# Other starting bytes in SBUF for the operands of 14,600 matmuls

## The chip, the core and the metric

The kernel runs on one core of a Trainium2 chip. The metric is the device time of one execution in microseconds. Of the kernel before there are three such times, 2232.58, 2233.57 and 2234.03 us; their median is 2233.57 us. A profiled execution gives the trace from which all rows below are read; its first to last instruction take 2229.6 us.

## The reference, cut to what matters

Two transformer blocks of two layers each run over the same 256 tokens of 1,024 values. Almost all the arithmetic is products of the activations with weight matrices that are used once:

```
def swiglu(x, w_gu, w_down):
    gate, up = jnp.split(x @ w_gu, 2, axis=-1)
    return (jax.nn.silu(gate) * up) @ w_down

def memory_cross_attention(x, mem, wq, wkv, wo):
    q = (x @ wq).reshape(B_, S, X_HEADS, X_HEAD_DIM) * (X_HEAD_DIM ** -0.5)
    k, v = jnp.split(mem @ wkv, 2, axis=-1)
    ...
    return o.reshape(B_, S, D_MODEL) @ wo
```

The first block has an mLSTM and neighbourhood mixer (layer 0), a differential attention (layer 1), and in each layer a cross attention and a SwiGLU of 2,816 hidden units. Each layer of the second block has a SwiGLU, a mixer of three branches with gates (the name merge in the code), a cross attention and a second SwiGLU. Layer norm with a residual stands after each of the 14 sublayers. All is in float32.

## The kernel before, in words

**Split operands.** TensorE multiplies at its fast rate in a float32 variant (F32R) with fewer bits. To keep accuracy, each operand is held as a high part and a low part: xh and xl are the transposed activations of a sublayer's input, hh and hl those of the hidden units, oh and ol those of an attention's or mixer's output, mh and ml those of the memory, yh and yl those of the three branches. A weight tile of 2,048 values a partition (8,192 bytes, 1 MB in all) comes by DMA into one of three buffers `raw`, ScalarE rounds it into `wh` (line 1260), VectorE writes what is left over into `wl` (line 1813), and TensorE makes three matmuls of each product (helper `three`, lines of `mm`, line 359): high by low, low by high, high by high. wh and wl have three buffers each, which are given back by the semaphore weights_used.

**What moves and what stands.** In proj_T the weights are the stationary operand (128 columns are loaded) and the activations move, 256 columns an instruction. In y_products (the second matrix of a SwiGLU, the output projections) and in proj_N it is the other way round: 128 columns of the activations stand, and 512 (or 256) columns of weights move. In enter, the first tiles of a next sublayer, the activations x stand and 256 or 512 columns of early weight tiles move; those tiles lie in front_h/front_l, in oh/ol (slot "side"), in hh/hl ("back"), or in em_h/em_l and en_h/en_l ("mem", "note", "under"). In a row of the profile `bank<-xl,wh 128x256` is a matmul of xl with wh by 256 moving columns.

**The order.** It is written out by hand: each engine's program calls the same sublayers in the same order, and semaphores join them. Nothing in it depends on addresses.

**Where tensors lie.** SBUF is given out in the order of the calls of sb: each tensor begins where the one before ends, and tensors named gap_... take only room. Tensors in an ExitStack that is closed share their room with what follows. The list begins at byte 16,512 of a partition, which is 128 past a multiple of 2,048 and of 512. From this and from the sizes the homes follow. Below, "remainder" is the starting byte of a tensor modulo 512. Every split tensor's inner steps are multiples of 512 bytes, so that each matmul operand in it starts at the tensor's own remainder.

## Time and profile before

| what | us |
|---|---|
| median of three runs | 2233.57 |
| span of the profiled execution | 2229.6 |
| what lies around the span (the difference) | 4.0 |
| TensorE busy with matmuls | 2202.7 |
| VectorE busy | 1434.7 |
| ScalarE busy | 1074.2 |
| GpSimd busy | 118.6 |

The profiled execution gives only a span; its own whole time is not recorded apart from it, so the 4.0 us are taken as lying around every span. Busy time of TensorE is a union: a matmul of 256 columns is shown as 276 ns long, but the next starts some 113 ns after it. For this kernel the distance from start to start is thus what costs, and it is read by dividing a stretch by its number of matmuls.

### The profile page before, as it was taken

What the parts mean: (1) busy time and instruction counts of PE and PEld (TensorE: products, weight loads), DVE (VectorE), ACT (ScalarE), POOL (GpSimd) and SP (SyncE); (2) the same over time, 40 slices, a digit from 0 to 9 for tenths busy, and PEclk for the clock granted to TensorE, in tenths of its full rate; (3) what the DMA queues carried; (4) which work ended last, traced back from release to release, by engine and by line L of the source; (5) the groups of instructions that cost most, each with busy time, mean ns of one, the idle gap of its engine ahead of it and who ended that gap; (6) DMA issues with size and microseconds to landing.
All of it is one profiled execution on the core that took longest, in us unless ns stands there. A gap on an engine that the chain in (4) does not pass through costs nothing.

```text
span 2229.6 us, 38285 instructions
## 1 busy us (share of the span) xinstructions
PE 2202.7 (99%) x16049; PEld 2048.8 (92%) x16049; DVE 1434.7 (64%) x1675; ACT 1074.2 (48%) x1317; POOL 118.6 (5%) x206
## 2 busy tenths in 40 slices
PE   9999999999999999999999999999999999999998
PEld 9989899888989989998999998998998999998997
DVE  6885655577655555556876676566556776677555
ACT  4554444357454443443556454444443555555442
POOL 2310000020000000000011000000000002000000
PEclk9999999999999999999999999999999999999999
DMA  7656556674645665566454655565565555465553
GB/s 244 213 186 208 169 175 191 203 200 153 208 151 181 198 226 171 189 218 197 151 159 145 198 196 179 193 217 180 189 200 193 180 164 160 153 234 163 189 180 123
DMA packets 349547, 413.93 MB, mean 186 GB/s; under 512 B 11964, under 2 KB 281464, under 8 KB 349248
## 3 DMA queue, kind: packets, MB, share of 16 engines
q1 hardware_dynamic: 339184, 377.19, 52.6%
q0 software_dynamic: 10192, 34.29, 4.8%
q8 instruction: 129, 2.11, 0.4%
q14 instruction: 42, 0.34, 0.0%
HBM read 406.44 MB, written 5.00 MB: 185 GB/s over the span
## 4 chain that ended last, share of the span: by engine, by line
PE 94%; DVE 3%; ACT 1%; issue 1%; DMA 0%; POOL 0%; DVEq 0%; ACTq 0%
PE bank L359 94%; DVE x L1927 0%; DVE z L1922 0%; DVE stat L1888 0%; DVE front_l L1813 0%; DVE z L1886 0%; PE bank L1226 0%; ACT wh L1260 0%; DMA lamt<-in_odd_lambda 0%; DVE em_l L1813 0%; ACT em_h L1260 0%; PE bank L1230 0%; DMA rx<-rs 0%; DVE xl L1847 0%; DVE nmax L2277 0%
## 5 line engine op out<-in xcount | busy, mean ns | idle before, releaser
L1813 DVE TENSOR_TENSOR wl<-raw,wh 128x2048 fp32r<-128x2048 f32 (+1 forms) x344 | 761.2, 2218 | 507.2 <-ACT wh L1260 426.6
L359 PE MATMUL bank<-xl,wh 128*128 128x256 f32 x3144 | 877.3, 279 | 5.4 <-issue 4.7
L359 PE MATMUL bank<-xh,wl 128*128 128x256 f32 x3144 | 871.2, 277 | 0.0
L359 PE MATMUL bank<-xh,wh 128*128 128x256 f32 x3144 | 871.2, 277 | 0.0
L1260 ACT ACTIVATE wh<-raw 128x2048 fp32r<-128x2048 f32 (+1 forms) x344 | 636.7, 1855 | 316.5 <-PE bank L359 306.6
L359 PEld LDWEIGHTS bank<-xl,wh 128*128 128x128 f32 x3144 | 591.7, 188 | 12.5 <-issue 10.5
L359 PEld LDWEIGHTS bank<-xh,wl 128*128 128x128 f32 x3144 | 591.2, 188 | 0.6
L359 PEld LDWEIGHTS bank<-xh,wh 128*128 128x128 f32 x3144 | 591.5, 188 | 0.2
L359 PE MATMUL bank<-wl,hh 128*128 128x512 f32 x528 | 205.9, 390 | 0.0
L359 PE MATMUL bank<-wh,hh 128*128 128x512 f32 x528 | 205.5, 389 | 0.0
L359 PE MATMUL bank<-wh,hl 128*128 128x512 f32 x528 | 205.5, 389 | 0.0
L1448 ACT ACTIVATE gate_s<-bank 128x512 f32<-128x512 f32 x54 | 32.4, 600 | 180.7 <-PE bank L359 180.7
L359 PEld LDWEIGHTS bank<-wh,hh 128*128 128x128 f32 x528 | 99.1, 188 | 20.7
L359 PEld LDWEIGHTS bank<-wh,hl 128*128 128x128 f32 x528 | 99.1, 188 | 20.3
L359 PEld LDWEIGHTS bank<-wl,hh 128*128 128x128 f32 x528 | 99.1, 188 | 20.0
L359 PE MATMUL bank<-wl,oh 128*128 128x512 f32 x224 | 89.7, 400 | 1.8 <-DVE ol L2268 1.6
L359 PE MATMUL bank<-wh,oh 128*128 128x512 f32 x224 | 87.4, 390 | 0.0
L359 PE MATMUL bank<-wh,ol 128*128 128x512 f32 x224 | 87.3, 390 | 0.0
L2546 POOL DMA_DIRECT2D gb<-in_ln_g x14 | 7.6, 543 | 1369.0 <-DVE x L1927 1362.1
L1291 ACT ACTIVATE xh<-bank 128x512 fp32r<-128x512 f32 x56 | 30.8, 600 | 73.3 <-PE bank L359 73.0
L1318 ACT ACTIVATE mv<-mv 128x1 f32<-128x1 f32 x28 | 5.7, 203 | 121.4 <-DVE mv L1914 121.4
L1886 DVE SCALAR_TENSOR_TENSOR z<-x,bank 128x512 f32<-128x512 f32 x56 | 38.3, 684 | 31.4 <-PE bank L359 30.9
(393 smaller groups left out, 3154.5 us busy)
## 6 DMA issues: line engine op xcount, KB each, us to landing
raw<-in_ffn_w_in SPq DMA_DIRECT2D x80, 1024.0 KB, 5.2
raw<-in_w_mix_in SPq DMA_DIRECT2D x56, 1024.0 KB, 5.3
raw<-in_ffn_w_gu SPq DMA_DIRECT2D x40, 1024.0 KB, 5.2
raw<-in_ffn_w_out SPq DMA_DIRECT2D x40, 1024.0 KB, 5.1
raw<-in_ffn_w_down SPq DMA_DIRECT2D x20, 1024.0 KB, 5.1
raw<-in_mem_wkv SPq DMA_DIRECT2D x16, 1024.0 KB, 5.4
raw<-in_even_w_in SPq DMA_DIRECT2D x13, 1024.0 KB, 6.8
raw<-in_w_branch SPq DMA_DIRECT2D x24, 512.0 KB, 3.5
```

The source lines that it names most:

```text
L359: ins = pe.transpose(o, a, b) if transpose else pe.matmul(o, a, b, start=start, stop=stop)
L1260: act.activation(part_of(t, 0), raw_tile(t), ACT.Copy).then_inc(sig("w_high"), 1)
L1291: act.activation(dst, src, ACT.Copy).then_inc(sig("part_high"), 1)
L1318: act.activation(mv[:, t, 2:3], mv[:, t, 1:2], ACT.Sqrt).then_inc(sig("std_ready"), 1)
L1448: free(("gate", j, q), act.activation(gate_s[:, q % 2, :], o[:, :], ACT.Silu))
L1813: dve.tensor_tensor(part_of(t, 1), raw_tile(t), part_of(t, 0).bitcast(F32), ALU.subtract)\
L1886: free(name, dve.scalar_tensor_tensor(z[:, t, f], x[:, t, f], ALPHA / c, o[:, :], ALU.mult, ALU.add))
L2546: pool.dma_start(gb[:, i, :], v.partition_broadcast(P)).then_inc(sig("gains_loaded"), 16)
```

## The change

Only calls of sb are changed: gap tensors are resized, put in or taken out, and seven small tensors move in front of the weights. No instruction is added, removed or moved: of the 21,600 instructions of the built program, on all engines, none differs in its operation, its shape, its operands' names, its offset inside them, or its semaphores. Line numbers below the change shift by two. The highest byte in use rises by 64.

| tensors | remainder by 512 before | after |
|---|---|---|
| wh, wl (all three buffers) | 128 (640 by 2,048) | 0 (0 by 2,048) |
| xh, xl | 64 | 448 |
| hh, hl | 128 | 0 |
| mh, ml; em_h, em_l, en_h | 64 | 0 |
| oh, ol | 128 | 64 |
| en_l | 128 | 64 |
| front_h, front_l | 128 | 0 |
| yh, yl | 64 | 128 |
| raw | 128 | 64 |
| x, z | 128 | 128 |

```
-    sb("gap_xh", [P, 112])
+    sb("gap_xh", [P, 80])
...
-    sb("gap_oh", [P, 16])
+    sb("gap_oh", [P, 32])
...
     raw = sb("raw", [P, RAW, TILE])
+    ident = sb("ident", [P, P])
+    pc = sb("pc", [P, P])
+    stat = sb("stat", [P, TB, 4, 6])
+    mv = sb("mv", [P, TB, 4])
+    nmax = sb("nmax", [P, 2, 4])
+    psum_e = sb("psum_e", [P, 2, 4])
+    rden = sb("rden", [P, 2, 4])
+    sb("gap_wh", [P, 32])
     wh = sb("wh", [P, PARTS, TILE], F32R)
     wl = sb("wl", [P, PARTS, TILE], F32R)
     gb = sb("gb", [P, 2, D])
-    ident = sb("ident", [P, P])
...
-    pc = sb("pc", [P, P])
-    stat = sb("stat", [P, TB, 4, 6])
-    mv = sb("mv", [P, TB, 4])
-    nmax = sb("nmax", [P, 2, 4])
-    psum_e = sb("psum_e", [P, 2, 4])
-    rden = sb("rden", [P, 2, 4])
...
-    sb("gap_hh", [P, 48], F32, st)
...
-    sb("gap_mh", [P, 32], F32, st)
...
-    sb("gap_em", [P, 32], F32, st)
```

The parts of the kernel that the diff touches, and what calls them:

Of the kernel before, what the change touches and what calls it, by code (L numbers as in the profile page):

```python
# [7 lines left out]
F32 = mybir.dt.float32  # L8
# [5 lines left out]
P = 128  # L14
# [3 lines left out]
TB = S // P  # L18
# [63 lines left out]
def program(nc, ctx, A, out, LAST=14):  # L82

    def sb(name, shape, dt=F32, on=None):
        return (on or ctx).enter_context(nc.sbuf_tensor(name, shape, dt))
# [4 lines left out]

    x = sb("x", [P, TB, D])
    z = sb("z", [P, TB, D])
    sb("gap_xh", [P, 112])
    st = ExitStack()
    mem_x = sb("mem_x", [P, TB, D], F32, st)
    st.close()
    xh = sb("xh", [P, KC, S], F32R)
    xl = sb("xl", [P, KC, S], F32R)
    sb("gap_oh", [P, 16])
    st = ExitStack()  # L100
    btab = sb("btab", [8, 512], F32, st)
    st.close()
    st = ExitStack()
# [2 lines left out]
    oh = sb("oh", [P, KC, S], F32R)  # L106
    ol = sb("ol", [P, KC, S], F32R)
    raw = sb("raw", [P, RAW, TILE])
    wh = sb("wh", [P, PARTS, TILE], F32R)
    wl = sb("wl", [P, PARTS, TILE], F32R)  # L110
    gb = sb("gb", [P, 2, D])
    ident = sb("ident", [P, P])
    ones = sb("ones", [P, P])
    st = ExitStack()
    front_h = sb("front_h", [P, TILE], F32R, st)
# [2 lines left out]
    st = ExitStack()  # L118
# [3 lines left out]
    probT = sb("probT", [P, 2, 512])  # L122
    logit = sb("logit", [P, 2, 512])
    bm = sb("bm", [P, 2, 512])
    pc = sb("pc", [P, P])
    stat = sb("stat", [P, TB, 4, 6])
    mv = sb("mv", [P, TB, 4])
    nmax = sb("nmax", [P, 2, 4])
    psum_e = sb("psum_e", [P, 2, 4])
    rden = sb("rden", [P, 2, 4])  # L130


    st = ExitStack()
    sb("gap_hh", [P, 48], F32, st)
    hh = sb("hh", [P, HC, S], F32R, st)
    hl = sb("hl", [P, HC, S], F32R, st)
    gate_s = sb("gate_s", [P, 2, 512], F32, st)
    hid = sb("hid", [P, 2, 512], F32, st)
    st.close()
    st = ExitStack()  # L140
    sb("gap_mh", [P, 32], F32, st)
    mh = sb("mh", [P, KC, S], F32R, st)
    ml = sb("ml", [P, KC, S], F32R, st)
    mem_n = sb("mem_n", [P, TB, D], F32, st)
# [2 lines left out]
    xv = sb("xv", [P, TB, D], F32, st)  # L147
    st.close()
    st = ExitStack()
    sb("gap_em", [P, 32], F32, st)  # L150
    em_h = sb("em_h", [P, TILE], F32R, st)
    em_l = sb("em_l", [P, TILE], F32R, st)
    en_h = sb("en_h", [P, TILE], F32R, st)
# [3 lines left out]
    st = ExitStack()  # L157
# [23 lines left out]
    st = ExitStack()  # L181
# [3 lines left out]
    st = ExitStack()  # L185
# [12 lines left out]
    st = ExitStack()  # L198
# [23 lines left out]
    st = ExitStack()  # L222
# [2515 lines left out]
```

## Rows read from the trace of the kernel before

**Rows 1.** Busy time of each engine, and the chain that ended last, by engine.
```profile
PE 2202.7 (99%) x16049; PEld 2048.8 (92%) x16049; DVE 1434.7 (64%) x1675; ACT 1074.2 (48%) x1317; POOL 118.6 (5%) x206
...
PE 94%; DVE 3%; ACT 1%; issue 1%; DMA 0%; POOL 0%; DVEq 0%; ACTq 0%
```

**Rows 2.** Busy time (instructions), clock, DMA share, GB/s in three stretches.
```profile
core 0: us, PE busy (x) PEld busy (x) DVE busy (x) ACT busy (x) POOL busy (x), PEclk, DMA share, GB/s
277.80:375.90 98.10, 98.10 (x868) 98.10 (x867) 51.26 (x34) 43.30 (x36) 0.00 (x0) 1.00 0.59 187
162.30:184.80 22.50, 22.50 (x192) 22.49 (x191) 17.61 (x17) 9.29 (x8) 1.10 (x2) 1.00 0.83 278
382.00:440.00 58.00, 58.00 (x259) 47.99 (x258) 33.65 (x28) 23.36 (x16) 0.00 (x0) 1.00 0.68 218
```

**Rows 3.** Tile xh, from 277.7 to 375.9: duration ns min/median/max, first and last start.
```profile
L359 PE MATMUL bank<-xh,wl x288: 276/276/279, 277.9 to 375.5; 128*128 128x256 f32 x144
```

**Rows 4.** Tile xh in a slow stretch, from 217.4 to 223.2.
```profile
L359 PE MATMUL bank<-xh,wl x16: 281/281/281, 217.8 to 223.1; 128*128 128x256 f32 x16
L359 PE MATMUL bank<-xh,wh x15: 281/281/281, 217.9 to 222.9; 128*128 128x256 f32 x15
```

**Rows 5.** Tile mh from 162.2 to 184.8, and from 1980 to 1991.
```profile
L359 PE MATMUL bank<-mh,wl x64: 281/281/281, 162.4 to 184.7; 128*128 128x256 f32 x64
...
L359 PE MATMUL bank<-mh,wl x30: 281/281/281, 1980.7 to 1990.9; 128*128 128x256 f32 x30
```

**Rows 6.** Tile yh, from 1221 to 1235.
```profile
L359 PE MATMUL bank<-yh,wl x42: 276/276/276, 1220.8 to 1234.7; 128*128 128x256 f32 x42
```

**Rows 7.** 512 moving columns: tile hh 384.5:440, oh 245:252, mh 151.2:162.2, xh 39:45.
```profile
L359 PE MATMUL bank<-wl,hh x81: 389/389/389, 384.6 to 439.0; 128*128 128x512 f32 x81
...
L359 PE MATMUL bank<-wl,oh x11: 389/389/389, 245.1 to 251.9; 128*128 128x512 f32 x11
...
L359 PE MATMUL bank<-wl,mh x16: 392/392/392, 151.3 to 161.6; 128*128 128x512 f32 x16
L359 PE MATMUL bank<-wh,mh x16: 388/388/389, 151.8 to 162.1; 128*128 128x512 f32 x16
...
L359 PE MATMUL bank<-wh,ml x16: 394/394/394, 151.6 to 161.8; 128*128 128x512 f32 x16
...
L359 PE MATMUL bank<-wl,xh x8: 397/398/400, 39.7 to 44.6; 128*128 128x512 f32 x8
```

**Rows 8.** x standing, 256 columns moving: tiles em_h, front_h 258:277.8; ol 845:857.
```profile
L359 PE MATMUL bank<-em_h,xh x16: 281/283/283, 258.8 to 272.0; 128*128 128x256 f32 x16
...
L359 PE MATMUL bank<-front_h,xh x16: 278/279/279, 266.7 to 277.7; 128*128 128x256 f32 x16
...
L359 PE MATMUL bank<-ol,xh x8: 279/279/279, 853.5 to 856.0; 128*128 128x256 f32 x8
```

**Rows 9.** Groups with shapes apart: busy us, mean ns, idle before.
```profile
L359 PE MATMUL bank<-xh,wl 128*128 128x256 f32 x3136 | 869.0, 277 | 0.0
L1813 DVE TENSOR_TENSOR wl<-raw,wh 128x2048 fp32r<-128x2048 f32 x321 | 734.4, 2292 | 486.0 <-ACT wh L1260 405.6 <-issue 79.7
L359 PE MATMUL bank<-wl,hh 128*128 128x512 f32 x528 | 205.9, 390 | 0.0
L359 PE MATMUL bank<-wl,oh 128*128 128x512 f32 x224 | 89.7, 400 | 1.8 <-DVE ol L2268 1.6
L359 PE MATMUL bank<-mh,wl 128*128 128x256 f32 x192 | 54.0, 281 | 0.0
L359 PE MATMUL bank<-yh,wl 128*128 128x256 f32 x192 | 53.0, 276 | 0.0
```

**Rows 10.** Who waited for whom: TensorE's longest, ScalarE's longest (us, times, longest).
```profile
PE bank L359 <- DVE x L1927: 7.2, 10, 1.4
...
ACT wh L1260 <- PE bank L359: 306.6, 119, 4.4
```

**Rows 11.** DMA issues of weights: count, KB each, median us to landing.
```profile
raw<-in_ffn_w_in SPq DMA_DIRECT2D x80, 1024.0 KB, 5.2
```

## The prediction

> **What bounds the kernel now.** I read the page's busy times and chain first. TensorE is busy 2202.7 of 2229.6 us and is 94% of the chain that ended last [rows 1]: only 26.9 us of the span are not matmuls. The granted clock is 1.00 in every stretch that I cite [rows 2], the level of 2.4 GHz, so it explains no difference below. Next I asked what a matmul costs from start to start. In the SwiGLU from 277.8 to 375.9 us, 98.10 us hold 868 matmuls, nearly all of 256 columns: 113 ns each. In the memory projection, 22.50 us hold 192 matmuls of the same shape: 117 ns each [rows 2]. The tile views say the same more sharply: 288 matmuls xh,wl, every third one, start between 277.9 and 375.5 us, which is 97.6/287/3 = 113.4 ns, each shown as 276 ns long [rows 3]; 64 of mh,wl start between 162.4 and 184.7, 22.3/63/3 = 118.0 ns, each shown as 281 ns long [rows 5]. So 5 ns more of shown duration go with 4.6 ns more from start to start, and the shown durations tell which of the two rates a stretch has.
>
> This is all that a change of addresses could move on the bounding engine, and there is little of it. Above the best rate stand:
> - x moving, weights standing (3 x 3,136 matmuls [rows 9]): most are at 276, but some whole tiles of 48 matmuls are at 281 [rows 4]. Tile by tile in the same view I count about 21 of these, some 1,000 matmuls: 1,000 x 4.6 ns = 4.6 us.
> - m moving: all 3 x 192 at 281 [rows 5, 9]: 2.6 us.
> - x standing, 256 columns moving (tiles of em, en, front, o, h): 279 to 283 [rows 8], some 900 matmuls at about 4.6 ns: 4.1 us.
> - 512 columns moving over m or x: 392, 394 and 388 for the three products where hidden and output tiles show 389 [rows 7], mean about 2.3 ns more; 288 and 240 matmuls: 1.2 us. A few tiles over x show 398; 0.5 us for them.
>
> The sum is 13.0 us, 0.6% of the time. That is the most that the change can win on TensorE if 276 and 389 are the floor, as the 8,400 and 1,500 matmuls that sit exactly there suggest.
>
> **The change part by part.** No instruction, wait or DMA is added, removed or moved, so every term is an unchanged count times a possible difference of spacing. The durations are of the profiled execution; its span is 2229.6 us, and 4.0 us lie around it to the median of 2233.6, so a term in the span is a term in the time.
>
> What decides between 276 and 281? The starting bytes alone don't. x over w and m over w have the same remainders by 512, 64 moving over 128 standing, and the same by 2,048, yet m is always slow and x mostly fast [rows 3, 5]. And x over w itself has both rates: a tile right behind another keeps its rate, while a tile that follows transposes or attention products may start in the other [rows 4]. I read this as two streams, the moving one and the load of the next stationary operand, that settle in one of two phases; addresses may shift the odds. Nothing here shows the absolute remainders apart from the distance of the two operands, so I take each new pair by the row that has the same distance (standing minus moving, by 512):
>
> - **x over w**: 64 before, 64 after (0 minus 448). Same distance, so the same odds of the two phases. The 21 slow tiles are spread by what ran before them, and that doesn't change. I take -1.0 us, a fifth of the 4.6, for phases that fall anew. Bounds: -4.6 (all fast), and 8,400 x 4.6 ns = +39 us (all at the rate of rows 5).
> - **w over h**: 0 before and after; 1,584 matmuls at 389. 0. Bounds: 0 and, at the rate of w over m, +3.6.
> - **w over o**: 0 to 64; 672 matmuls. No row has 512 columns at 64; w over m has minus 64 and 2.3 ns more. I take half of 672 x 2.3 = 1.5, so +0.8. Bounds -0.3 and +1.5.
> - **w over m**: minus 64 to 0, the distance of w over h: 288 x 2.3 ns = -0.7. Bounds -0.7 and 0.
> - **m over w**: 64 to 0. At 256 columns distance 0 is em over x, at 283, two more than now: 576 x 2 = +1.2; at 512 columns it is the fast one, -2.6. I take -0.7, the middle.
> - **y over w**: 64 to minus 128, which no row has. 576 matmuls, all at 276 now [rows 6, 9]. Bounds 0 and +2.6 (281); I take +0.5.
> - **x standing, 256 moving**: em goes from 0 to minus 64, the distance of front over x, which shows 279 against 283 [rows 8]: 256 x about 3 ns = -0.8. front keeps minus 64. o goes from minus 64 to minus 128, unknown, 96 matmuls, at most 0.5 either way. Together -0.8. Bounds -4.1 and +1.5.
>
> The sum is -1.0 + 0 + 0.8 - 0.7 - 0.7 + 0.5 - 0.8 = -1.9 us.
>
> The other engines read and write at new bytes too. VectorE's split of a tile takes 2292 ns [rows 9] and ScalarE's less, while TensorE spends 48 x 113.4 = 5,440 ns on the tile; in the SwiGLU VectorE is busy 51.26 and ScalarE 43.30 of 98.10 us [rows 2], and ScalarE waits 306.6 us in all for TensorE to give back a buffer before it splits [rows 10]. A split 10% longer stays hidden. A DMA lands 5.2 us after its issue [rows 11], at a DMA share of 0.59 with three buffers of raw; a tenth more is hidden too. Where it is not hidden, at the end of a sublayer, VectorE's norm stands in the chain for 3% of the span, 67 us; 1% of that would be 0.7 us, which I leave at 0.
>
> Hence 2229.6 - 1.9 + 4.0 = 2231.7 us. About 0.2%, 4.5 us, is what a measurement of this kernel can tell from no change, so this forecast is called no change.
>
> A rule of the Trainium skill bears on this. Its page "TensorE: Matmul & The Clock Gate", in "LDWEIGHTS — get the stationary operand into the array", says in my words that TensorE has two independent read ports of SBUF, so that loading the next stationary operand takes nothing from the running matmul. By it homes would not matter at all, and the time would be 2233.6. The trace doesn't settle it: rows 3 and 5 differ in spacing at one shape and one clock, so something beside shape decides, and that may be phase alone.
>
> **The rivals.**
>
> *All operands fall in the fast phase.* For it: 276 and 389 are sharp, common and reached by several pairs, and each new pair with w, h and m has both operands at whole multiples of 512, which no pair has now. Against it: x over w keeps its distance, and its slow tiles come after pauses. It wins between half and all of the 13.0 us: 2223 us, taking 10.5.
>
> *The long chains of x over w take the slow phase.* The price is 4.6 ns for each matmul that changes sides, and 8,400 could. From about an eighth of them, 1,000 or 21 tiles more, the kernel is slower by more than 4.5 us; if a quarter of the fast ones switches it is +9.7, and if all do +39. For it: m over w has the very remainders and distance of x over w and is always slow [rows 5], so the fast phase is not guaranteed by them; and a moving x at 448 crosses the next multiple of 512 after 64 bytes, where now it crosses after 448. Against it: the six SwiGLUs run their chains of 18 tiles at 113.4, entered from slow stretches of front over x, so the fast phase seems to draw them in. Smaller losses in y, o and m, up to 6 us together, join it. I price it at a quarter: 2243 us.
>
> *The change doesn't do what it says*, since homes have no part in the rates at all: then even the small terms vanish, 2233.6 us, also no change.
>
> **How the numbers follow.** No change holds 0.41: 0.28 for the small sum around 2231.7 and 0.13 for homes without influence. The fast rival holds 0.35, the slow one 0.24. The likeliest is the small sum, 2231.7; its own range is 2229 to 2236. The range for 8 in 10 goes down to 2221, which takes in nearly all of the fast rival (its full 13.0 us would be 2220.6), and up to 2246, which takes in the slow one up to a third of the chains.
>
> **What would show it.** The durations in the tile views answer each step: xh,wl in the SwiGLUs at 276 (281 or more: the slow rival); the 21 slow tiles still about as many (none: the fast rival); mh,wl away from 281; w over m at 389 throughout; em over x nearer 279; y still at 276. The forecast is wrong if a pair shows a spacing below 113 ns, which no row has now and which would break the floor; if VectorE's 2292 or ScalarE's duration changes by more than a tenth and turns up in TensorE's waits; or if the DMAs land late and the chain shows them.

## The result, and the profile after

| | before | after |
|---|---|---|
| median of 5 runs each, us | 2232.58 (2229.42 to 2234.03) | 2239.96 (2238.99 to 2240.46) |
| ratio | 1 | 1.0039, 95% interval 1.0028 to 1.0050 |
| span of the profiled execution, us | 2229.6 | 2237.2 |
| TensorE busy, us | 2202.7 | 2210.0 |

The change makes the kernel slower: by 7.4 us between the medians (0.33%), by 0.39% in the ratio on record, which is not the ratio of the two medians. The forecast was 2231.7 us, no change. All of the loss is on TensorE: its busy time grows by 7.3 us and the span by 7.6. The first two parts of the page after, against [rows 1]:

```profile
PE 2210.0 (99%) x16049; PEld 2053.4 (92%) x16049; DVE 1434.4 (64%) x1675; ACT 1073.1 (48%) x1317; POOL 118.3 (5%) x206
...
PE 91%; DVE 4%; issue 2%; ACT 2%; DMA 0%; POOL 0%; DVEq 0%; ACTq 0%
```

VectorE, ScalarE and GpSimd have the busy times of before within 1.1 us. TensorE's share of the chain is 91% where it was 94%, but its busy share stays 99% and no other engine works longer, so no new bound shows; at which steps the chain took another path I did not follow up.

The granted clock is no cause of it. While matmuls run it falls three times in each of the two spans to 0.50, the level of 1.2 GHz, for 3.4 us, the first time behind 8.8 us in which TensorE was busy for 6.77. The two stretches of before, then the first fall of after (window; busy us and instructions of PE, PEld, DVE, ACT, POOL; clock, DMA share, GB/s):

```profile
1100.00:1108.80 8.80, 6.77 (x61) 6.50 (x60) 4.66 (x6) 5.16 (x7) 0.00 (x0) 1.00 0.22 78
1108.80:1112.20 3.40, 3.40 (x18) 3.40 (x18) 3.40 (x5) 2.84 (x3) 0.97 (x2) 0.50 0.75 223
...
1110.30:1113.70 3.40, 3.40 (x19) 3.40 (x18) 3.40 (x6) 1.98 (x2) 1.43 (x2) 0.51 1.01 319
```

In such a stretch matmuls of 256 columns start 213 ns apart and not 113, so one costs about 1.6 us (16 x 0.1, an estimate). The traces of the experiments have between one such stretch (e8, e10) and five (e6, where two follow each other at once). Much of what the times of one kernel differ by is this, and it has to be kept apart from the rates that are the subject here.

The groups with shapes apart (busy us, mean ns, idle before; lines stand two lower than before) answer to [rows 9]:

```profile
L357 PE MATMUL bank<-xh,wl 128*128 128x256 f32 x3136 | 869.6, 277 | 0.0
L1811 DVE TENSOR_TENSOR wl<-raw,wh 128x2048 fp32r<-128x2048 f32 x321 | 734.4, 2292 | 489.7 <-ACT wh L1258 407.7 <-issue 80.3 <-PE bank L357 0.8
L357 PE MATMUL bank<-wl,hh 128*128 128x512 f32 x528 | 205.9, 390 | 0.0
L357 PE MATMUL bank<-wl,oh 128*128 128x512 f32 x224 | 90.7, 405 | 1.8 <-DVE ol L2266 1.6
L357 PE MATMUL bank<-mh,wl 128*128 128x256 f32 x192 | 54.3, 283 | 0.0
L357 PE MATMUL bank<-yh,wl 128*128 128x256 f32 x192 | 54.0, 281 | 0.0
```

The landing of the weights (count, KB, us), against [rows 11], and ScalarE's longest wait, against [rows 10]:

```profile
raw<-in_ffn_w_in SPq DMA_DIRECT2D x80, 1024.0 KB, 5.3
```

```profile
ACT wh L1258 <- PE bank L357: 307.9, 118, 4.4
```

The split takes 2292 ns as before, the weights land 0.1 us later, and the wait for buffers grows by 1.3 us in 307. Only matmuls changed: wl,oh from 400 to 405 in the mean, mh,wl from 281 to 283, yh,wl from 276 to 281, and hidden tiles not at all. The tile views show the same without the mixing of a mean (duration min/median/max, first and last start; they answer to [rows 3, 5 to 8]):

```profile
L357 PE MATMUL bank<-xh,wl x288: 276/276/281, 277.5 to 375.8; 128*128 128x256 f32 x144
...
L357 PE MATMUL bank<-wl,mh x16: 389/389/389, 149.9 to 160.1; 128*128 128x512 f32 x16
...
L357 PE MATMUL bank<-mh,wl x63: 283/283/283, 161.2 to 183.6; 128*128 128x256 f32 x63
...
L357 PE MATMUL bank<-wl,oh x12: 394/394/394, 245.0 to 252.7; 128*128 128x512 f32 x12
...
L357 PE MATMUL bank<-yh,wl x62: 279/281/285, 1218.0 to 1240.5; 128*128 128x256 f32 x62
...
L357 PE MATMUL bank<-em_h,xh x16: 279/280/280, 258.0 to 271.3; 128*128 128x256 f32 x16
...
L357 PE MATMUL bank<-xh,wl x32: 281/281/281, 196.6 to 207.5; 128*128 128x256 f32 x32
```

The last row has its answer in a row of before that did not stand ahead of the prediction: the same two tiles of x, the first behind a memory-value product.

```profile
L359 PE MATMUL bank<-xh,wl x32: 276/276/281, 197.8 to 208.4; 128*128 128x256 f32 x32
```

Where did 7.6 us go? I took pairs of neighbouring matmuls of one kind (the same sort of moving and of standing operand, the same number of columns) and summed the time from start to start above a floor of 113.3 ns (256 columns) and 226.7 ns (512 columns). This sum is my own working from the start times of the trace. A pair counts if it lies within 12 ns of its floor in both traces, so waits and the stretches at half the clock are left out; 13,857 pairs are left. Where a single trace is spoken of below, the same is summed in it alone (before 14.0, after 22.8 us).

| moving over standing | pairs | before, us | after, us | difference |
|---|---|---|---|---|
| x over w | 9239 | 5.15 | 7.00 | +1.9 |
| w over h | 1565 | 0.15 | 0.15 | 0.0 |
| w over o | 624 | 0.62 | 4.12 | +3.5 |
| y over w | 560 | 0.06 | 3.02 | +3.0 |
| m over w | 572 | 2.56 | 3.80 | +1.2 |
| w over m | 272 | 0.67 | 0.19 | -0.5 |
| em over x | 215 | 1.31 | 0.95 | -0.4 |
| all, with the smaller ones | 13857 | 13.85 | 22.69 | +8.8 |

These pairs are 8.8 us longer. All other stretches of TensorE (waits, transposes, attention products) are 1.1 us shorter and those at half the clock 0.1 us shorter, which leaves the 7.6 us of the span. So the question is not where the time went but what gives a pair of homes its rate.

### The profile page after: what moved, and what is told of

It reads as the page before. It is cut to its first block, busy times and chain, and to the rows that moved or that the text cites. A ratio compares the mean times of both kernels' runs of the same rounds, so it can differ in the third digit from the quotient of the medians.

```text
span 2237.2 us, 38285 instructions
## 1 busy us (share of the span) xinstructions
PE 2210.0 (99%) x16049; PEld 2053.4 (92%) x16049; DVE 1434.4 (64%) x1675; ACT 1073.1 (48%) x1317; POOL 118.3 (5%) x206
## 4 chain that ended last, share of the span: by engine, by line
PE 91%; DVE 4%; issue 2%; ACT 2%; DMA 0%; POOL 0%; DVEq 0%; ACTq 0%
PE bank L357 91%; ACT prob L1765 1%; ACT wh L1258 1%; DVE x L1925 0%; DVE nmax L2467 0%; DVE z L1920 0%; DVE stat L1886 0%; DVE front_l L1811 0%; DVE logit L2464 0%; DVE z L1884 0%; PE bank L1224 0%; DMA rx<-rs 0%; DVE wl L1811 0%; DVE em_l L1811 0%; ACT em_h L1258 0%
```

## The experiments

The theory in them: the rate of a pair depends on the distance of its two operands, standing home minus moving home. Its rivals: each home's own bytes, larger powers of two (1,024 or 2,048 bytes), or the kind of work. The distance is given as what is left of it after whole multiples of 512 bytes, further down of 256. Later a second theory joined: a matmul takes over a state from the one ahead of it. In the edits `sb` places the next tensor, and a gap of n moves all behind it by 4n bytes.

### Everything moved together: e1_shift_all

```
@@ kernel before @@
+    sb("gap_all", [P, 96])
     x = sb("x", [P, TB, D])
```

> The kernel before with every tensor moved up by 384 bytes: all distances between operands are those of before, while the starting bytes modulo 512 of w, x, y and o become those of the changed kernel or nearly (w 0, x 448, o 0, h 0, m 448, y 448). Theory distance (the spacing depends on standing minus moving operand, modulo 512): every pair keeps its duration (w over o and w over h 389, m over w 281, y over w 276, em over x 283), the time is that of before within 0.1%. Theory absolute (the remainders themselves decide): x over w has the bytes of the changed kernel and takes its share of 281 (about 460 of each 3,144 instead of 330), and o or y leave 389 or 276: 2 to 9 us slower.

Measured: 2231.55 us, ratio to before 0.9996 (0.9987 to 1.0005), span 2229.0. The rows of e1:

```profile
L360 PE MATMUL bank<-mh,wl x63: 281/281/281, 162.6 to 184.5; 128*128 128x256 f32 x63
...
L360 PE MATMUL bank<-xh,wl x288: 276/276/279, 278.1 to 375.7; 128*128 128x256 f32 x144
```

Every home has another remainder by 512 and by 2,048, and every pair of this list keeps its duration; the sum over all pairs is 13.7 us against 14.0. The remainders by themselves have no part in it, as far as a move by 384 bytes tells; only what two homes are to each other is left.

### One pair put back at a time: e2_o_back, e3_y_back, e4_m_back

```
@@ e2: kernel after @@
-    sb("gap_oh", [P, 32])
+    sb("gap_oh", [P, 16])
-    sb("gap_wh", [P, 32])
+    sb("gap_wh", [P, 48])
@@ e3: kernel after @@
+    sb("gap_yh", [P, 80], F32, st)
@@ e4: kernel after @@
+    sb("gap_hh", [P, 128], F32, st)
+    sb("gap_mh", [P, 112], F32, st)
+    sb("gap_em", [P, 112], F32, st)
-    sb("gap_en", [P, 3 * 2048 + 1040], F32, st)
+    sb("gap_en", [P, 3 * 2048 + 1040 - 112], F32, st)
```

> The changed kernel with oh and ol at the distance 0 from the weights again (remainder 0, not 64). Theory distance: w over o goes back from 394 to 389, which is 672 matmuls at about 5 ns: 3.4 us faster than the changed kernel, 1.0023 times the kernel before. Rival, that w over o is slow because the weights now lie at a multiple of 2,048: w over o stays at 394, and the time stays at 1.0039.

> The changed kernel with yh and yl at 448, the distance 64 from the weights as before. Theory distance: y over w goes back from 279 to 285 to 276 in nearly all its 576 matmuls, 3.0 us faster than the changed kernel, 1.0026 times the kernel before. Theory absolute: 448 is no byte that y had before, so nothing says that it gets 276; it stays slow.

> The changed kernel with mh and ml, and the early tiles em and en_h, at 448: the distances of before (64 for m over w, minus 64 for w over m, 0 for em over x). Theory distance: m over w goes back from 283 to 281 (-1.3 us), w over m from 389 to the 392, 394, 388 of before (+0.6), em over x from 279 to 283 (+0.4): in sum -0.3 us against the changed kernel, no difference that can be timed, but all three durations visible in the trace. Theory absolute: m and em at 448 show durations that neither kernel has.

Measured, against before at 2232.13 us: e2 2236.74 (ratio 1.0019, 1.0010 to 1.0028), e3 2235.73 (1.0016, 1.0007 to 1.0025), e4 2237.79 (1.0019, 1.0010 to 1.0028). Tile rows of e2, then e3, then e4:

```profile
L357 PE MATMUL bank<-wl,oh x14: 389/389/389, 242.9 to 251.7; 128*128 128x512 f32 x14
```

```profile
L358 PE MATMUL bank<-yh,wl x40: 276/276/282, 1218.8 to 1232.9; 128*128 128x256 f32 x40
```

```profile
L360 PE MATMUL bank<-wl,mh x16: 397/397/398, 150.9 to 161.4; 128*128 128x512 f32 x16
...
L360 PE MATMUL bank<-mh,wl x62: 276/276/281, 162.9 to 183.8; 128*128 128x256 f32 x62
...
L360 PE MATMUL bank<-xh,wl x32: 276/276/281, 196.9 to 207.4; 128*128 128x256 f32 x32
```

With o at distance 0 again wl,oh is back at 389, and the sum of w over o falls from 4.1 to 0.6 us. With y at distance 64 again yh,wl is back at 276, 3.0 to 0.1 us, and the gate tiles of x between the y tiles go back to 276 as well. As e1 has ruled out the remainders by themselves, each of these two losses hangs on its pair's distance.

e4 was a surprise. It gives m over w its old distance, so 281 was expected, and it shows 276, better than either kernel (3.8 to 0.1 us). The run ahead of it, wl,mh, is at 397 instead of 392, though its distance is also the old one. So distance alone doesn't fix the rate; something carried over from the work ahead has a part in it. The two tiles of x behind w over m are at 276 again. In the trace the total gained little, 1.4 us, because w over m itself rose from 0.2 to 1.0 us and x over w from 7.0 to 8.3. The ratios of e3 (1.0016 where 1.0026 was expected) and e4 (1.0019 where hardly less than after's 1.0039 was) look better than that; the last part of this section says why they should not be read so.

### Larger powers of two: e5_w_1024, e6_m_1024, e7_x_o_back

```
@@ e5: kernel before; ident and ones from behind wl to here, so w, o and raw 1,024 bytes on @@
+    ident = sb("ident", [P, P])
+    ones = sb("ones", [P, P])
     sb("gap_oh", [P, 16])
@@ e6: kernel before; m, h and em 1,024 bytes on @@
-    sb("gap_hh", [P, 48], F32, st)
+    sb("gap_hh", [P, 48 + 256], F32, st)
-    sb("gap_mh", [P, 32], F32, st)
+    sb("gap_mh", [P, 32 + 256], F32, st)
-    sb("gap_em", [P, 32], F32, st)
+    sb("gap_em", [P, 32 + 256], F32, st)
@@ e7: kernel after; the block of small tensors ahead of xh, o at distance 0 @@
-    sb("gap_xh", [P, 80])
+    ident = sb("ident", [P, P])
...
+    sb("gap_xh", [P, 128])
-    sb("gap_oh", [P, 32])
+    sb("gap_oh", [P, 16])
```

> The kernel before with o, raw and the split weights moved up by 1,024 bytes: every distance to the weights modulo 512 stays, modulo 2,048 it changes by 1,024 (x over w from 64 to 1,088, m over w the same). Theory 512 (only the distance modulo 512 counts, and which of two rates a pair at distance 64 takes is chance): m over w stays at 281 and x over w keeps about 330 of 3,144 at 281; the time is that of before. Theory 2,048 (the distance counts modulo 2,048, since in the changed kernel with m put back m over w was at 1,088 and ran at 276 and not at the 281 of before): m over w goes to 276, 2.6 us less, and the share of x over w at 281 changes, by up to 2 us either way; w over h, now at a distance of 1,024, may leave 389 as well.

> The kernel before with mh, ml, the early tiles em, en_h and hh, hl moved up by 1,024 bytes: x over w keeps its distance of 64 also modulo 2,048, m over w goes to 1,088. Theory 2,048: m over w at 276, 2.6 us faster than before (ratio 0.9988), x over w as before. Theory of inheritance (m over w takes its rate from the stretch of w over m ahead of it, whatever the multiple): m over w follows w over m, which keeps its distance modulo 512, so 281 and no gain. Theory 512: nothing changes.

> The changed kernel with o back at distance 0 and x back at the distance that it had modulo 2,048 (64, not 1,600); its remainder by 512 stays 448. Beside the run that put back o alone it tells what x over w cost. Theory 2,048: x over w loses some 180 of each 3,144 matmuls at 281, 540 x 4.6 = 2.5 us less than with o back alone, so about 1.0008 times before (y and m still cost 3.0 + 1.2 - 0.5 - 0.4 us, which gives 1.0015). Theory chance: x over w stays between 440 and 540 at 281 for each product, and the time is that of the run with o back, 1.0019.

Measured, against before at 2231.42 us: e5 2232.49 (ratio 1.0003, 0.9994 to 1.0013), e6 2231.63 (1.0002, 0.9993 to 1.0011), e7 2235.82 (1.0022, 1.0013 to 1.0031). The rows of e5, e6 and e7:

```profile
L359 PE MATMUL bank<-mh,wl x63: 281/281/281, 162.9 to 184.8; 128*128 128x256 f32 x63
```

```profile
L359 PE MATMUL bank<-mh,wl x63: 281/281/281, 162.4 to 184.3; 128*128 128x256 f32 x63
```

```profile
L356 PE MATMUL bank<-wl,oh x13: 389/389/389, 243.3 to 251.4; 128*128 128x512 f32 x13
```

With 1,024 bytes between the homes added on one side or the other, m over w stays at 281. For this pair a rule in 1,024 or 2,048 is refuted. x over w did not stand still: 6.5 us in e5 and 5.7 in e6, where before has 5.2. In both, three tiles of x behind a run of 512 columns (at 456 us) went from 276 to 281, though all distances by 512 are those of before, and in e6 x and w have not moved at all. So the distance does not fix the rate of x over w; whether the 1,024 bytes or chance changed it, one trace of each cannot tell. e7 keeps the distances of e2 while xh stands at 1,984 by 2,048 instead of 448 and o at 0 instead of 512; it has the rates of e2 (x over w 7.3 us against 7.9, where the theory of 2,048 asked for 2.5 less), and its time within the intervals.

### Distances that no row had: e8_y_384, e10_y256_m320, e11_y320_m256

```
@@ kernel before; e8: 96, e10: 80, e11: 64 @@
+    sb("gap_yh", [P, 96], F32, st)
@@ e10: + 64, e11: + 80 in gap_mh and gap_em @@
-    sb("gap_hh", [P, 48], F32, st)
+    sb("gap_hh", [P, 48 + 128], F32, st)
-    sb("gap_mh", [P, 32], F32, st)
+    sb("gap_mh", [P, 32 + 64], F32, st)
```

> The kernel before with yh and yl moved up by 384 bytes, so that weights stand 192 ahead of the moving y, not 64; all else stays. Theory distance: y over w leaves 276, as it did at minus 128 in the changed kernel; 192 has no row yet, the cost lies between 0 and 4 us. Theory absolute: y at 448 (the byte at which it ran at 276 in the changed kernel with y put back) over w at 128 runs at 276 again, and the time is that of before.

> A look for a distance with one fast rate only: the kernel before with y at distance 256 from the weights (not 64) and m at 320, so that w over m is at 192 (hh keeps its distance 0). By the rows so far 0, 192, 384 and 448 all show more than 276 at 256 columns, so both theories expect none below 276; a distance opposite to the others may show 276 with no second rate, which the twelve m tiles, entered from different stretches, would tell. If the distance matters only when it is within 192 bytes of 0, both y at 256 and m at 320 are at 276.

> The same with the two exchanged: y at distance 320, m at 256 (w over m at 256 too). Theory distance: m shows what y showed at 256 in the run before and y what m showed at 320; theory of the tile (each tensor has its own rate by what runs around it): they don't exchange.

Measured: e8 2232.36 us (ratio to before 1.0008, 0.9999 to 1.0017). In e8 the gate tiles of x between those of y go to 281 as well. e10 and e11 had one timed run each, 2233.92 and 2241.23 us, with before at 2233.43. The rows of e8, of e10 and of e11:

```profile
L360 PE MATMUL bank<-yh,wl x44: 279/279/279, 1219.7 to 1234.9; 128*128 128x256 f32 x44
```

```profile
L360 PE MATMUL bank<-yh,wl x43: 280/283/283, 1219.8 to 1234.9; 128*128 128x256 f32 x43
...
L360 PE MATMUL bank<-mh,wl x64: 281/281/281, 162.5 to 184.7; 128*128 128x256 f32 x64
```

```profile
L360 PE MATMUL bank<-yh,wl x41: 276/276/282, 1220.5 to 1234.9; 128*128 128x256 f32 x41
...
L360 PE MATMUL bank<-mh,wl x62: 282/283/283, 162.7 to 184.6; 128*128 128x256 f32 x62
```

y at 256 does what em over x does at 0 (283); y at 320 what it does at 64 (276); m at 320 stays at 281, as at 64; m at 256 goes to 283, as at 0. e8 has y at 192 and shows 279, as front over x at 448 does [rows 8]. The distance counts by 256 bytes and not by 512, in every pair tried. The last row that the table needs is of the kernel after, where early weights in oh move over x, which stands 384 bytes on:

```profile
L357 PE MATMUL bank<-oh,xh x8: 392/394/397, 445.1 to 454.8; 128*128 128x512 f32 x8
```

| distance by 256 | 256 columns, ns shown | 512 columns, ns shown |
|---|---|---|
| 0 | 283 | 389 |
| 64 | 276 or 281 | 394 (w over o) |
| 128 | 279 to 285 (y, after) | 392 to 397 (o over x, after) |
| 192 | 279, 280 | 392, 394, 388 in turn, or 397, 398 |

So no distance is best for both shapes: 0 is the floor with 512 moving columns and the worst with 256.

e11 brought something that nobody had asked for. Its one time is 7.8 us over the median of before, and its span 2239.4 us against 2229.6, 9.8 us more, where the pairs that it moves account for under 1 us. (One time alone would prove little: the 13 of before beside it include a 2240.82, at a mean granted clock of 0.994 where the others have 0.995 to 0.999. The rows of the trace decide.) Its window over the third SwiGLU (busy us and instructions of each engine, clock, DMA share, GB/s), and below it that of before:

```profile
873.00:974.60 101.60, 101.60 (x865) 101.60 (x864) 51.27 (x34) 43.16 (x36) 0.00 (x0) 1.00 0.57 181
```

```profile
871.50:969.20 97.70, 97.70 (x865) 97.70 (x863) 51.10 (x34) 43.30 (x36) 0.00 (x0) 1.00 0.59 188
```

The tile view of e11 in the third SwiGLU and in the first, each with the last matmul ahead of the chain:

```profile
L360 PE MATMUL bank<-xh,wl x288: 281/281/281, 873.0 to 974.4; 128*128 128x256 f32 x144
L360 PE MATMUL bank<-front_h,xh x1: 277/277/277, 872.8 to 872.8; 128*128 128x256 f32 x1
...
L360 PE MATMUL bank<-xh,wl x287: 276/276/281, 278.6 to 375.9; 128*128 128x256 f32 x144
...
L360 PE MATMUL bank<-front_h,xh x1: 281/281/281, 278.4 to 278.4; 128*128 128x256 f32 x1
```

865 matmuls take 101.60 instead of 97.70 us, at a clock of 1.00: a whole chain of 18 tiles, 864 matmuls of x over w, runs at 281. So does the sixth SwiGLU. x over w as a whole has 15.1 us above the floor where before has 5.2: 2 x 3.9 = 7.8 of the 9.9 are these two chains, 1.7 are the eight tiles behind w over m (as in after, below). x and w have the homes of before here. What differs is the entry: in the two slow chains the last matmul ahead, front_h,xh, shows 277 ns, in the four fast ones 281, and in all six of before 278. A chain keeps the rate that it is entered with, for 100 us. What changed the entry is not shown: the homes of front, x and w did not move.

### What is taken over: e9_o_m_back, e12_phase

e9 is the kernel after with the edits of e2 and e4 together. It differs from e4 in o's home alone.

> The changed kernel with both o and m (with em, en_h) back at the distances of before. It differs from the run that put m alone back only in o. There m over w ran at 276, though its distance was the 64 at which before it ran at 281. Theory inheritance (a pair at distance 64 keeps the rate in which it is entered, and the last matmuls of 512 columns ahead decide it: 389, 389, 389 or 392, 394, 388 lead into 281; 388, 392, 394 or 394, 388, 392 or 397s and 398s into 276): the four m over w tiles of the second block that follow w over o, now at 389 again, go back to 281, and the x over w tiles behind w over m stay at 276. Rival, that the bytes of m (448 over weights at 0) give 276: they stay at 276. Time: 1.0010 to 1.0020 times before (y still costs 3 us).

Measured: 2234.69 us (ratio to before 1.0007, 0.9997 to 1.0017). The rows of e9:

```profile
L360 PE MATMUL bank<-mh,wl x60: 281/281/281, 162.3 to 183.1; 128*128 128x256 f32 x60
...
L360 PE MATMUL bank<-xh,wl x31: 276/276/281, 196.6 to 206.8; 128*128 128x256 f32 x31
```

m over w is back at 281 in all its tiles, w over m back at 392, 394 and 388, with no home of either moved from e4; the tiles of x behind stay at 276. That speaks for a state handed on from earlier matmuls, but o has moved. e12 moves no home at all. It leaves out matmuls of the run ahead of m over w: one in the first of the two places, three in the second, so the output misses four products.

```
@@ kernel before; leave is 1 at k == 6 of the first run, 3 at k == 6 of the second @@
         def three(o, ah, al, bh, bl, first, last, full=None, leave=0):
+            if leave == 3:
+                return
             mm(o, ah, bl, first, False)
-            mm(o, al, bh, False, False)
+            if leave == 0:
+                mm(o, al, bh, False, False)
             mm(o, ah, bh, False, last, full)
```

> The kernel before with no home moved. In the two places where a run of memory-key products (tile mh or ml moving, wh or wl standing, 192 matmuls of 256 columns) follows a run of memory-value products (512 columns, wh or wl moving, mh or ml standing), matmuls of 512 columns are left out one k step before the end of that run: in the first place one (a correction product), in the second three (all products of that k step), so the output misses these. Theory (a matmul at distance 64 takes over one of two spacings, and which one depends on where in its cycle of three, 392, 394, 388 ns, the run ahead of it stops): leaving out one stops the cycle at another point, leaving out three does not. So in the first place the memory-key products go from 281 to 276 ns, 192 of them, about 0.8 us less; in the second place they stay at 281. Rival A (the spacing belongs to the pair of homes, 281 for memory over weights): both stay at 281. Rival B (each pair of tiles has its own value in the run ahead, wh over ml 394 and so on, and no cycle is taken over): leaving out one changes nothing in the first place either. With the 4 matmuls of 227 ns left out (0.9 us) the theory expects 1.7 us less than before plus or minus what the x tiles behind do, a ratio of about 0.9992; the rivals 0.9 us less, 0.9996. The durations of the rows decide, not the time.

Measured, against before at 2231.91 us: 2230.19, ratio 0.9992 (0.9983 to 1.0001), span 2227.8. The tile views of e12, at the first place in three stretches (well ahead of the matmul left out, around the end of the run, and behind it), then at the second place:

```profile
L359 PE MATMUL bank<-wl,mh x7: 392/392/392, 155.7 to 159.8; 128*128 128x512 f32 x7
L359 PE MATMUL bank<-wh,mh x6: 388/388/388, 156.2 to 159.6; 128*128 128x512 f32 x6
...
L359 PE MATMUL bank<-wh,mh x2: 393/394/394, 160.7 to 161.4; 128*128 128x512 f32 x2
L359 PE MATMUL bank<-wl,mh x1: 388/388/388, 161.0 to 161.0; 128*128 128x512 f32 x1
...
L359 PE MATMUL bank<-mh,wl x59: 276/276/279, 162.5 to 182.7; 128*128 128x256 f32 x59
...
L359 PE MATMUL bank<-wh,mh x2: 388/388/389, 570.5 to 571.2; 128*128 128x512 f32 x2
L359 PE MATMUL bank<-wl,mh x1: 392/392/392, 570.8 to 570.8; 128*128 128x512 f32 x1
...
L359 PE MATMUL bank<-mh,wl x63: 281/281/281, 571.6 to 593.5; 128*128 128x256 f32 x63
```

One matmul left out, and the values 392, 394, 388 go to other tiles: wl,mh turns from 392 to 388, wh,mh from 388 to 394. They belong to a cycle of three and not to the pairs of tiles, so rival B falls. The 192 matmuls behind go from 281 to 276, so rival A falls. Three left out, and cycle and rate stay as before. This is the control: less work ahead is not what does it. There was one place of each kind, and one trace. The sum of m over w falls from 2.56 to 1.74 us. The time agrees with the 1.7 us expected, but its interval also holds no change; the durations decide.

The last three durations ahead tell the rate that follows wherever a tile at distance 64 comes right behind 512 columns, in all 106 such places of the 14 traces (values within 1 ns): 392, 394, 389 and 389 three times lead to 281; 388, 392, 393, also 394, 388, 397 or 398, and what ends a run at 392 or 397 (392, 392, 396; 397, 397, 392; 398, 393, 397) lead to 276. The SwiGLUs behind front agree: 280, 279, 278 (before, all six) and 279, 280, 281 (e11, four) lead to 276; 279, 279, 277 (e11, two) to 281. This is an observation over these kernels, made after the fact, and not a mechanism.

The times can be set beside the traces if each is taken times its mean granted clock, an estimate of what it would be at a clock of 1.00; the clock is on record to 0.001, which is 2.2 us, so only medians of many are of use. The table has the median of this minus the median for the runs of before beside it (2224.5 to 2226.0 us; for after, whose runs of before have no clock on record, 2224.9 over all 94), in us, and the sum over all pairs of the trace minus that of before:

| kernel | from the times | from the trace |
|---|---|---|
| after (5 times) | +8.8 | +8.8 |
| e1, everything moved | -0.1 | -0.3 |
| e2, o back | +5.8 | +6.0 |
| e3, y back | +5.5 | +6.7 |
| e4, m back | +8.3 | +7.4 |
| e5, e6 (1,024 bytes) | -0.3, +0.2 | +1.4, +0.6 |
| e7, x and o back | +6.4 | +5.4 |
| e8, y at 192 | +4.1 | +3.9 |
| e9, o and m back | +2.6 | +4.7 |
| e10, e11 (one time each) | +3.5, +10.7 | +5.2, +10.4 |

The two agree within 2.1 us everywhere. So the spacing in the traces is what the times consist of, e8's 0.9 us between medians hid about 4, and e4's better ratio was clock and not rates. e12 has 1.3 us less by its times and 0.9 by its trace, which does not count the four matmuls left out.

## Why the forecast was wrong

Right in it: only TensorE's spacing could move; the other engines, the waits and the DMAs stayed; the shown duration tells the rate; the distance of the two homes matters and their own bytes don't (e1). The rule cited from the Trainium skill (page "TensorE: Matmul & The Clock Gate", section "LDWEIGHTS — get the stationary operand into the array") is that loading the next stationary operand takes nothing from the running matmul. If homes did not matter, as the forecast read it, the time would not have changed. The measurement decides against that reading: 7.4 us in the medians, and e2 and e3 tie 3.5 and 3.0 us to the distances of two pairs. That it is reading which the two operands disturb is not shown.

Step by step:

- **w over o**, +0.8 with a bound of +1.5, measured +3.5. The step that failed: "No row has 512 columns at 64; w over m has minus 64 and 2.3 ns more." That row is at another distance, 192 by 256, and was taken for its mirror. The real one shows 394 on all three products and is 5.6 ns slower than before (3.5 us over 624 pairs), so the bound was less than half of what came. This is the term that left its bounds by most.
- **y over w**, +0.5, measured +3.0. The mechanism was allowed for, and a little more than its upper bound of +2.6 is what came; I had taken a fifth of it only because 276 was its rate before. At 128 bytes the shown values change between 279 and 285.
- **m over w**, -0.7, measured +1.2. Two prices stood side by side, +1.2 from the row with 256 columns at distance 0 [rows 8] and -2.6 from 512 columns at distance 0. The row of the same shape was right to a tenth, and averaging it with a row of another shape was the error.
- **x over w**, -1.0, measured +1.9. "Same distance, so the same odds" failed because the odds hang on what runs ahead. The eight tiles right behind w over m went to 281 when w over m went to 389, and four gate tiles behind y went with y: 12 x 48 x 4.5 ns = 2.6 us. The other slow stretches of x became fewer, 816 matmuls where before has 1,056, which is -1.1 us. They stand behind other work, where the rate also changes between kernels that keep these distances (x over w is 5.2 us before, 4.8 in e1, 5.7 in e6, 6.5 in e5), so that part may be chance.
- **w over m**, -0.7, and **x standing**, -0.8: the signs were right, with -0.5, and -0.3 for its 256-column pairs.
- **The 4.0 us around the span**, taken from one span and a median of other executions. In every run of after and of the experiments, where both are on record, it is 1.8 us. The rest was the spread from one execution to the next; it put the forecast 2.2 us too high and is no part of the miss.

The terms of w over o, y over w and m over w sum to +0.6 in the forecast and to +7.7 in the trace, 7.1 of the 10.7 us between -1.9 and 8.8; x over w is 2.9 more.

The slow rival named x's long chains. After shows none (276 in the SwiGLU), so the loss came by what the forecast called "smaller losses in y, o and m, up to 6 us together"; they were 7.7. Yet its mechanism exists. The argument against it, that "the fast phase seems to draw them in", is refuted by e11, where two chains started at 281 and stayed there for all 864 matmuls. The fast rival is dead: its reason, whole multiples of 512 on both sides, is distance 0, and that is 389 for 512 columns but 283, the worst, for 256. The rival that homes have no part in the rates is refuted by e2 and e3.

What stays open: why one distance has two rates that keep themselves, and what sets the state behind transposes and attention products, which is behind the slow tiles of before [rows 4]. Each kernel has one trace, so how far the entries change from one execution to the next stays open too. The experiments point to a kernel with the homes of before and an entry like that of e12 for m over w; with the products kept it would gain 2.6 us at most (576 x 4.5 ns), under what a measurement of this kernel can tell, and it was not built.

## What to carry to other kernels

When TensorE is 99% busy and homes in SBUF are moved, write down for every pair that meets in a matmul the distance standing minus moving by 256 bytes, and look up its shown duration at the same number of moving columns; a row of another distance or shape is no price. A rate seen on one stretch belongs to that stretch's entry as much as to its homes, so a change in one product can reprice the untouched run behind it, and a chain of 100 us can turn as a whole. The largest difference here, e11 against before, is 9.8 us of the span, 0.4%: worth a check at the end of tuning, with the rest of the trace held still. Before times that differ so little are compared, look at the granted clock of each.

## What the runs showed of the hardware

- At one clock (1.00) and one shape, 256 moving float32r columns, matmuls start 113.3, 117.8 or 119.9 ns apart and show 276, 281 or 283 ns; 512 columns start 226.7 ns apart (389 shown), 229.2 in the mean of the cycle 392, 394, 388, and 233.3 at 394.
- Which of them depends on the distance between the homes by 256 bytes (e2, e3, e8, e10, e11), and not on the homes' own remainders (e1) or, for m over w, on 1,024 (e5, e6).
- At distance 64 two rates keep themselves, 276 and 281, over 864 matmuls in a row (e11), and a single 512-column matmul left out ahead turned 192 from one to the other (e12).
- In stretches of 3.4 us the granted clock is 0.50 (1.2 GHz), one to five of them in a trace while matmuls run; matmuls of 256 columns start 213 ns apart there, and each stretch costs about 1.6 us, an estimate.
